# Five spreads of 128 slot rows for seven of 96, and earlier parameter loads, in a two-block transformer kernel

## The chip, the cores and the metric

The kernel runs on one core of a Trainium2 chip, in one launch. The metric is the device time of that launch in microseconds; a smaller number is better. The program is written at the level of the engines' own instruction streams: TensorE (PE) for matmuls, VectorE (DVE), ScalarE (ACT), GpSimd (POOL), and SyncE (SP), whose queue issues the loads of weights. Semaphores tie the streams together.

## The reference

Two blocks of two layers each, in float32, on 256 tokens of width 1024. The first block's layer 0 is a matrix-memory mixer (mLSTM, 4 heads of width 512) with a gated feed-forward, its layer 1 a state-space mixer (S5) with a mixture of 8 experts. The second block has latent attention and a recurrent mixer, each with a gated feed-forward. What the change touches, cut to the core:

```python
def s5_mixer(u, lam_re, lam_im, b_re, b_im, c_re, c_im, d_skip, log_dt, w_glu, b_glu):
    dt = jnp.exp(f32(log_dt))[:, None]
    mag = jnp.exp(lr * dt)
    ar, ai = mag * jnp.cos(li * dt), mag * jnp.sin(li * dt)
    ...
    bbar_re = kr[..., None] * br - ki[..., None] * bi
    ...

def moe_ffn(u, w_router, w13, w2):          # 8 experts, top 2, F = 2816
    logits = (t @ w_router).astype(jnp.float32)
    top_val, top_idx = lax.top_k(logits, TOP_K)
    top_w = jax.nn.softmax(top_val, axis=-1)
    for e in range(N_EXPERTS):
        gate_e = jnp.sum(jnp.where(top_idx == e, top_w, 0.0), axis=-1)
        out = out + gate_e[:, None] * swiglu(t, w13[e], w2[e])
```

## The kernel before, in words

The whole is one long program, stage after stage; activations stay in on-chip memory and 565 MB of weights and inputs stream in once. SyncE loads weight tiles of up to 1 MB into a ring of 6 buffers. The load of a tile waits until TensorE has begun the tile five places before it (`tile_begun`, in `load`). TensorE's order is written out by hand, as is every other engine's.

**The end of the mLSTM and the first feed-forward.** `stage_mlstm` on ScalarE ends with `head_squares` and `head_root` for the last head (L2178 to L2190) and `layer_norm(0)`, whose squares are L2095. VectorE scales each head's output (L2780) and multiplies it (L2783, which signals `h_scaled`). TensorE meanwhile runs the output projection (L1286). `stage_ffn0` on ScalarE (L2203) waits for the first normalized input, issues nine loads (router, B, C and log_dt of the S5 layer, L2206 to L2215), and takes the silus of steps 0 and 1 (L2115). Then `s5_exponentials` (L2192) waits for all nine loads and exchanges values with a chain of small VectorE operations (L2836 to L2869). Only after it come the silus of the later steps. VectorE, too, runs that chain ahead of the product of step 2 (L2638). A step of the feed-forward is 64 matmul records of gate and up (L980) and 32 of the down projection (L1134); the down projection of step s stands behind the gate and up of step s + 1.

**The experts.** `stage_moe` gives each expert 96 slots (`SLOTS`) for the tokens that chose it. `xe` holds the gathered tokens, `wgather` the weight of each token in each slot. TensorE turns `wgather` into `scatterT`, slots on the partitions (L1467), and ScalarE copies it (L2285). If no expert has more than 96 tokens, `few_tokens` runs: the 176 hidden chunks of 128 (22 for each expert) go in 44 quads. A quad has four gate and up tiles (`gate_up`, L1481), three turns of the hidden values (`turn_hidden`, L1492) and two down tiles (`down`, L1505). In each, TensorE's four strips of 32 columns hold 32 slots each, so an expert's output stands as 3 rounds of slots by 4 quarters of the width. ScalarE copies it out (`y_quarters`, L2294) and issues 12 small copies (L2310) that bring it into `ye`, with 96 slot rows on the partitions. One quad later `spread` (L1518) multiplies each of the 8 column chunks of `ye` by the expert's `scatterT`, and VectorE adds the result to `res` (L3054). At expert 0 ScalarE also issues 12 copies of the last expert's scatter matrix (L2305), so that the last expert can be spread straight from `y_quarters` (L1542), with 32 slot rows in each of the array's four strips of rows. In every quad ScalarE's order is: three silus (L2316), the outputs of an expert that has ended, the copy of the turned hidden values (L2320), for which the next down product waits.

A number such as L1481 is the line in the code below. One matmul of the program stands as two records in the trace.

## Time and profile before

| | |
|---|---|
| median of 3 runs | 2809.24 us (2805.33 to 2809.74) |
| the profiled execution, its own time | 2807.94 us |
| its span, first to last instruction | 2806.2 us |
| TensorE busy (matmuls) | 2694.8 us, 96% of the span |
| VectorE, ScalarE, GpSimd busy | 786.1, 404.3, 763.0 us |
| transferred | 565.39 MB, 201 GB/s over the span |
| granted TensorE clock, mean | 0.976 |

The profile is of one execution. All times in its rows are counted from the first instruction. The span is 1.7 us less than the execution's own time, which is what the runs' times are. Busy time of TensorE runs to modelled ends of matmuls, so two groups that follow each other can overlap by a few tenths; where a length matters, starts are subtracted. The granted clock is a share of 2.4 GHz.

### The profile page before, as it was taken

How to read it: one execution, taken by the hardware profiler on the slowest of the kernel's cores; microseconds unless marked ns; L12 is line 12 of the kernel's file. 1: busy time of each engine (PE TensorE's matmuls, PEld its weight loads, DVE VectorE, ACT ScalarE, POOL GpSimd, SP SyncE). 2: the span in 40 equal slices, each digit the busy share in tenths (PEclk: the TensorE clock that was granted, in tenths of full speed). 3: DMA queues.
4: the chain of work that ended last, by engine and by line, in shares of the span. 5: the costliest groups of instructions: out<-in, count | busy, mean ns of one | idle time of the engine just before them, and what ended most of it. 6: DMA issues, size and time to landing. Idle time of an engine off the chain costs nothing.

```text
span 2806.2 us, 52573 instructions
## 1 busy us (share of the span) xinstructions
PE 2694.8 (96%) x23411; PEld 1983.1 (71%) x23411; DVE 786.1 (28%) x1504; ACT 404.3 (14%) x828; POOL 763.0 (27%) x591
## 2 busy tenths in 40 slices
PE   7999999999999999999999898999999989999998
PEld 5756778866655566656655345468888868998998
DVE  3306310064300000000002286132220146432561
ACT  0032010120210000000002244110000031221100
POOL 0051018064000000000000161045555432521886
PEclk9999999989999999999999999999999999998999
DMA  9976444468599999999998320132222242222542
GB/s 305 309 266 229 135 144 150 150 211 306 176 335 368 367 374 384 378 382 382 381 378 301 87 83 1 60 120 91 85 81 83 87 131 94 72 76 76 166 159 98
DMA packets 375012, 565.39 MB, mean 201 GB/s; under 512 B 50136, under 2 KB 205440, under 8 KB 374656
## 3 DMA queue, kind: packets, MB, share of 16 engines
q1 hardware_dynamic: 351504, 554.58, 56.9%
q10 hardware_dynamic: 23280, 7.42, 1.2%
q8 instruction: 186, 3.05, 0.5%
q14 instruction: 42, 0.34, 0.0%
HBM read 557.75 MB, written 1.05 MB: 199 GB/s over the span
## 4 chain that ended last, share of the span: by engine, by line
PE 53%; issue 35%; DMA 3%; POOL 3%; DVE 2%; POOLq 2%; ACT 1%; ACTq 1%; DVEq 1%; SPq 0%
PE psum L980 10%; PE psum L1799 9%; PE psum L2017 5%; PE psum L1836 5%; PE psum L1880 3%; PE psum L1134 2%; PE psum L2045 2%; PE psum L1286 2%; PE psum L1900 2%; PE psum L1621 2%; DMA sv<-in_s_log_dt 2%; PE psum L1021 1%; DMA ring<-in_ada_w 1%; PE psum L1927 1%; POOLq L3600 1%
## 5 line engine op out<-in xcount | busy, mean ns | idle before, releaser
L1481 PE MATMUL psum<-ring,xe 128*32 128x256 f32 x8448 | 465.7, 379 | 1.9 <-issue 1.9
L1481 PEld LDWEIGHTS psum<-ring,xe 128*32 128x32 f32 x8448 | 271.2, 110 | 183.0 <-issue 10.3
L980 PE MATMUL psum<-act_in,ring 128*128 128x256 f32 x1216 | 268.6, 382 | 2.5 <-DVE act_in L2616 1.4
L980 PEld LDWEIGHTS psum<-act_in,ring 128*128 128x128 f32 x1216 | 231.2, 191 | 41.7 <-issue 9.1
L3599 POOL TENSOR_TENSOR cq<-cq,nstat 128x512 f32<-128x512 f32 x3 | 3.7, 1269 | 932.5 <-DVE nstat L3150 932.5
L1505 PE MATMUL psum<-ring,zs 128*32 128x256 f32 x4224 | 239.2, 382 | 4.6 <-ACT zs L2320 4.6
L3061 DVE TENSOR_TENSOR zs<-zs,psum 128x128 f32<-128x128 f32 x132 | 37.9, 288 | 632.3 <-ACT zs L2316 632.3
L1505 PEld LDWEIGHTS psum<-ring,zs 128*32 128x32 f32 x4224 | 138.8, 111 | 96.3 <-issue 7.6
L3612 POOL TENSOR_TENSOR w_sums<-ring 128x512 f32<-128x512 f32 (+1 forms) x34 | 42.2, 1242 | 307.2 <-DVE ctxT L3201 131.3
L1621 PE MATMUL psum<-a,ring 128*128 128x512 f32 x224 | 97.5, 594 | 2.0 <-ACT a L2362 1.3
L2316 ACT ACTIVATE zs<-psum 128x128 f32<-128x128 f32 x132 | 36.4, 278 | 389.4 <-PE psum L1481 389.4
L3150 DVE RECIPROCAL nstat<-nstat 128x512 f32<-128x512 f32 x23 | 76.8, 3345 | 48.7 <-ACT nstat L2086 48.2
L1799 PE MATMUL psum<-a,ring 128*128 128x256 f32 x352 | 82.2, 386 | 4.1 <-DVE a L3121 4.1
L1134 PE MATMUL psum<-zs,ring 128*128 128x256 f32 x352 | 80.3, 387 | 6.0 <-DVE zs L2638 6.0
L1799 PE MATMUL psum<-a,w_sums 128*128 128x256 f32 x352 | 85.0, 385 | 0.7 <-ACT a L2362 0.7
L980 PE MATMUL psum<-a,ring 128*128 128x256 f32 x384 | 83.9, 379 | 0.0
L1621 PEld LDWEIGHTS psum<-a,ring 128*128 128x128 f32 x224 | 42.1, 190 | 56.0 <-issue 51.8
L1799 PE MATMUL psum<-x_rows,w_sums 128*128 128x256 f32 x352 | 79.8, 380 | 0.0
L1134 PEld LDWEIGHTS psum<-zs,ring 128*128 128x128 f32 x352 | 68.4, 195 | 16.0 <-issue 6.4
L980 PEld LDWEIGHTS psum<-a,ring 128*128 128x128 f32 x384 | 72.6, 190 | 9.7
L1799 PEld LDWEIGHTS psum<-a,ring 128*128 128x128 f32 x352 | 67.6, 193 | 14.7 <-DVE a L3121 4.7
L1799 PEld LDWEIGHTS psum<-a,w_sums 128*128 128x128 f32 x352 | 67.9, 193 | 10.9 <-issue 1.4
(549 smaller groups left out, 4228.0 us busy)
## 6 DMA issues: line engine op xcount, KB each, us to landing
ring<-in_moe_w SPq DMA_DIRECT2D x320, 512.0 KB, 7.1
ring<-in_ffn_w SPq DMA_DIRECT2D x97, 1024.0 KB, 5.3
ring<-in_ada_w SPq DMA_DIRECT2D x96, 1024.0 KB, 8.1
ring<-in_moe_w SPq DMA_DIRECT2D x88, 1024.0 KB, 8.3
ring<-in_hg_w_in SPq DMA_DIRECT2D x20, 1024.0 KB, 5.2
ring<-in_mlstm_w_in SPq DMA_DIRECT2D x16, 1024.0 KB, 6.4
ring<-in_moe_w SPq DMA_DIRECT2D x64, 256.0 KB, 5.7
ring<-in_mlstm_w_out SPq DMA_DIRECT2D x8, 1024.0 KB, 5.7
```

Of the source, the lines that this page charges most:

```text
L980: last = pe.matmul(bank(j)[:, n * T:(n + 1) * T], tile[:, k * width + n * P:k * width + (n + 1) * P], src(k), start=start and k == 0, stop ...
L1134: last = pe.matmul(psum[:, NB + n // 2, (n % 2) * T:(n % 2 + 1) * T], ring[:, t % RING, k * D + n * P:k * D + (n + 1) * P], hid[:, i % 2, ...
L1286: last = pe.matmul(bank(j)[:, n * T:(n + 1) * T], ring[:, t % RING, k * 256 + n * P:k * 256 + (n + 1) * P], hT[:, 8 * half + k], start=hal ...
L1481: last = pe.matmul(psum[32 * g:32 * g + 32, r, 0:2 * P].rearrange("p (u n) -> p u n", u=2), xe[:, 2 * i + k, at:at + 32], tile[:, k, :, g ...
L1505: last = pe.matmul(psum[32 * b:32 * b + 32, DOWN + r // 2, (r % 2) * T:(r % 2 + 1) * T], q_hidT[:, q % 2, r, 32 * g:32 * g + 32], ring[:, ...
L1621: last = pe.matmul(bank(j), ring[:, t % RING, at:at + P], src(k), start=k == 0, stop=k == kc - 1)
L1799: last = pe.matmul(product_bank(side, m), held[:, k], moving(k), start=k == 0, stop=k == 3)
L1836: last = pe.matmul(product_bank(q, m), held[:, k, q], moving(2 * kk + k), start=kk == 0 and k == 0 and m in (1, 5, 3, 6), stop=kk == 5, sk ...
L1880: last = pe.matmul(product_bank(side, m), held[:, k], moving(k), start=k == 0, stop=k == 3)
L1900: last = pe.matmul(bank(j)[:, a * T:(a + 1) * T], a2[:, k, tok:tok + P], ring[:, t % RING, k * 256:(k + 1) * 256], start=k == 0, stop=k == ...
L2017: last = pe.matmul(small_bank(side, m), held[:, k], moving(k), start=k == 0, stop=k == 3)
L3150: dve.reciprocal(st, st).then_inc(S("nrstd_ready"), 1)
```

## The change

It does two things.

First, the nine loads for the S5 layer become a function `s5_loads` of their own, called on ScalarE ahead of `layer_norm(0)`, behind a wait for `h_scaled` of all four heads. `ctok` and `bT` exchange their addresses.

Second, the slot rows of all experts are counted through: 8 x 96 = 768 rows are 24 pieces of 32 and 6 chunks of 128. `scatterT` is turned as 6 chunks. The row pieces of experts 0 to 6 but the last one (`KEPT_ROWS` = 20) go to `ye`, now two buffers of 128 rows, and each of the 5 full chunks is spread once its last row has come: behind experts 1, 2, 3, 5 and 6 (`SPREAD_AFTER`). The piece of expert 6 that is left over stays with the three of expert 7 in `y_kept`, and the last spread takes these four pieces. The copies for that (`last_rows`) go out four at a time behind each of the first four quads.

On ScalarE, the end of the mLSTM and the start of the feed-forward. Before (`qk` holds the heads' outputs, `xm` the residual, `zs` the hidden values, `sv`, `ctok`, `bmat` the S5 parameters):

```order
L2190 ACTIVATE bd<-psum,one 128x256
L2095 ACTIVATE xm<-xm 128x512 x4
L2090 ACTIVATE stat<-psum 128x256
L2086 ACTIVATE small<-psum,one 128x2
L2206 DMA router_w<-in_moe_router 128x8x8
L2208 DMA bmat<-in_s_b_re 128x32x16
L2208 DMA bmat<-in_s_b_im 128x32x16
L2211 DMA ctok<-in_s_c_re 128x8x64 x2
L2211 DMA ctok<-in_s_c_im 128x8x64 x2
L2215 DMA sv<-in_s_log_dt 64x32x1 x2
L2115 ACT_TABLE_LOAD
L2115 ACTIVATE zs<-psum 128x512 x2
```

and with the change:

```order
L2214 ACTIVATE bd<-psum,one 128x256
L2193 DMA router_w<-in_moe_router 128x8x8
L2195 DMA bmat<-in_s_b_re 128x32x16
L2195 DMA bmat<-in_s_b_im 128x32x16
L2198 DMA ctok<-in_s_c_re 128x8x64 x2
L2198 DMA ctok<-in_s_c_im 128x8x64 x2
L2202 DMA sv<-in_s_log_dt 64x32x1 x2
L2102 ACTIVATE xm<-xm 128x512 x4
L2097 ACTIVATE stat<-psum 128x256
L2093 ACTIVATE small<-psum,one 128x2
L2122 ACT_TABLE_LOAD
L2122 ACTIVATE zs<-psum 128x512 x2
```

The loads have moved ahead of the four squares (`xm<-xm`) of the layer norm, and the two silus follow the norm directly.

On ScalarE in the experts, the first quads. Before, after six quads without a load:

```order
L2316 ACTIVATE zs<-psum 128x128 x3
L2320 ACTIVATE zs<-psum 128x384
L2316 ACTIVATE zs<-psum 128x128 x3
L2294 ACTIVATE zs<-psum 128x768
L2305 DMA last_scatter<-scatterT 32x256 x12
L2310 DMA ye<-zs 32x256 x12
L2320 ACTIVATE zs<-psum 128x384
L2316 ACTIVATE zs<-psum 128x128 x3
```

and with the change, the first two quads:

```order
L2333 ACT_TABLE_LOAD
L2333 ACTIVATE zs<-psum 128x128 x3
L2337 ACTIVATE zs<-psum 128x384
L2327 DMA last_scatter<-scatterT 32x256 x4
L2333 ACTIVATE zs<-psum 128x128 x3
L2337 ACTIVATE zs<-psum 128x384
L2327 DMA last_scatter<-scatterT 32x256 x4
```

and expert 0's end:

```order
L2333 ACTIVATE zs<-psum 128x128 x3
L2313 ACTIVATE zs<-psum 128x768
L2321 DMA ye<-zs 32x256 x12
L2337 ACTIVATE zs<-psum 128x384
L2333 ACTIVATE zs<-psum 128x128 x3
```

The loads of `last_scatter` stand four at a time behind the turned values' copy (128x384) of a quad, and no longer ahead of the rows' copies at expert 0's end.

On TensorE, the quad behind expert 0. Before:

```order
L1505 MATMUL psum<-ring,zs 32x256 x24
L1481 MATMUL psum<-ring,xe 32x256 x72
L1505 MATMUL psum<-ring,zs 32x256 x48
L1492 MATMUL psum<-cst,zs 128x128 x3
L1518 MATMUL psum<-scatterT,ye 128x256 x8
L1481 MATMUL psum<-ring,xe 32x256 x96
L1505 MATMUL psum<-ring,zs 32x256 x48
```

and with the change:

```order
L1510 MATMUL psum<-ring,zs 32x256 x24
L1486 MATMUL psum<-ring,xe 32x256 x72
L1510 MATMUL psum<-ring,zs 32x256 x48
L1497 MATMUL psum<-cst,zs 128x128 x3
L1486 MATMUL psum<-ring,xe 32x256 x96
L1510 MATMUL psum<-ring,zs 32x256 x48
```

The spread (`scatterT,ye`) of expert 0 is gone there; its rows are in the spread behind expert 1.

The diff, cut to its core:

```diff
+KEPT_ROWS = 3 * (NE - 1) - 1
+SPREAD_AFTER = {(4 * kk + 3) // 3: kk for kk in range(KEPT_ROWS // 4)}
...
+        ctok = sb("ctok", [P, 2, DC, 2, SP_], work)
         bT = sb("bT", [P, 2, DC, P], work)
-        ctok = sb("ctok", [P, 2, DC, 2, SP_], work)
         cmT = sb("cmT", [P, 2, DC, P], work)
...
-        scatterT = sb("scatterT", [P, NE, T], work)
+        scatterT = sb("scatterT", [P, NE * SLOTS // P, T], work)
         xe = sb("xe", [P, DC, NE * SLOTS], work)
-        ye = sb("ye", [P, D], work)
-        last_scatter = sb("last_scatter", [P, 3, T], work)
+        ye = sb("ye", [P, 2, D], work)
+        last_scatter = sb("last_scatter", [P, 4, T], work)
         crowded = work.enter_context(nc.sbuf_tensor("crowded", [P, 1], mybir.dt.int32))
         work.close()
...
+        y_kept = zflat[:, 12 * T:16 * T].rearrange("p (r n) -> p r n", r=4)
+        wgather_slots = wgather.rearrange("p a e s -> p a (e s)")
...
-                for g in range(4):
+                for g in range(3):
                     for i in range(2):
                         for a in range(2):
-                            at = i * T + a * P
-                            last = pe.transpose(psum[0:SLOTS, NB + g, at:at + P], wgather[:, a, 2 * g + i], ident)
+                            at, s0 = i * T + a * P, (2 * g + i) * P
+                            last = pe.transpose(psum[:, NB + g, at:at + P], wgather_slots[:, a, s0:s0 + P], ident)
                     last.then_inc(S("scatterT_full"), 1)
 
...
                     def spread(e):
-                        pe.wait_ge(S("moe_y_turned"), 16 * 12 * (e + 1))
+                        kk = SPREAD_AFTER[e]
+                        pe.wait_ge(S("moe_y_turned"), 64 * min(3 * (e + 1), KEPT_ROWS))
                         for g in range(4):
-                            pe.wait_ge(S("spread_out"), 4 * e + g + 1)
+                            pe.wait_ge(S("spread_out"), 4 * kk + g + 1)
                             for n in range(2):
                                 last = pe.matmul(psum[:, SPREAD + g % 2, n * T:(n + 1) * T],
-                                                 ye[0:SLOTS, (2 * g + n) * P:(2 * g + n + 1) * P],
-                                                 scatterT[0:SLOTS, e], start=True, stop=True)
+                                                 ye[:, kk % 2, (2 * g + n) * P:(2 * g + n + 1) * P],
+                                                 scatterT[:, kk], start=True, stop=True)
                             last.then_inc(S("spread_full"), 1)
 
                     for n, (kind, q, i) in enumerate(EXPERT_TILES):
...
+                    pe.wait_ge(S("last_scatter_in"), 16 * 16)
                     pe.wait_ge(S("moe_y_out"), NE)
-                    pe.wait_ge(S("spread_out"), 2 + 4 * (NE - 1))
-                    for r in range(3):
+                    pe.wait_ge(S("spread_out"), 2 + 4 * len(SPREAD_AFTER))
+                    for r in range(4):
                         for n in range(2):
                             for b in range(4):
                                 rows = slice(32 * b, 32 * b + 32)
-                                last = pe.matmul(psum[:, NB + b, n * T:(n + 1) * T], y_quarters[rows, r, n * P:(n + 1) * P],
-                                                 last_scatter[rows, r], start=r == 0 and n == 0, stop=r == 2,
+                                last = pe.matmul(psum[:, NB + b, n * T:(n + 1) * T], y_kept[rows, r, n * P:(n + 1) * P],
+                                                 last_scatter[rows, r], start=r == 0 and n == 0, stop=r == 3,
                                                  skip_group_check=True)
                     last.then_inc(S("last_spread"), 1)
 
...
                 head_root(NH - 1)
+                s5_loads()
                 layer_norm(0)
...
-            def stage_ffn0():
-
-                act.wait_ge(S("ffn0_in_ready"), 1)
+            def s5_loads():
+
+                act.wait_ge(S("h_scaled"), NH)
                 act.dma_start(router_w[:], w["moe_router"][0].rearrange("(c p) e -> p c e", p=P)).then_inc(S("s5_in"), 16)
                 for i, name in enumerate(("s5_b_re", "s5_b_im")):
                     act.dma_start(bmat[:, i], w[name][0].rearrange("(j g) p h -> (g p) j h", g=2)).then_inc(S("s5_in"), 16)
...
                     act.dma_start(sv[g * SP_:(g + 1) * SP_, 0], log_dt[g:g + 1].broadcast_to([SP_, NPAIR]),
                                  allow_slow_non_contiguous=True
                                  ).then_inc(S("s5_in"), 16)
...
-                for g in range(4):
+                for g in range(3):
                     act.wait_ge(S("scatterT_full"), g + 1)
-                    act.activation(scatterT[0:SLOTS, 2 * g:2 * g + 2],
-                                   psum[0:SLOTS, NB + g].rearrange("p (e t) -> p e t", e=2), ACT.Copy
+                    act.activation(scatterT[:, 2 * g:2 * g + 2],
+                                   psum[:, NB + g].rearrange("p (e t) -> p e t", e=2), ACT.Copy
                                    ).then_inc(S("scatterT_out"), 1)
...
 
                         act.wait_ge(S("moe_y_full"), e + 1)
-                        act.activation(y_quarters.rearrange("p r n -> p (r n)"),
-                                       psum[:, DOWN:DOWN + 2].rearrange("p b n -> p (b n)")[:, 0:3 * T], ACT.Copy
-                                       ).then_inc(S("moe_y_out"), 1)
+                        rounds = psum[:, DOWN:DOWN + 2].rearrange("p b n -> p (b n)")[:, 0:3 * T]
                         if e == NE - 1:
+                            act.activation(y_kept[:, 1:4].rearrange("p r n -> p (r n)"), rounds, ACT.Copy
+                                           ).then_inc(S("moe_y_out"), 1)
                             return
                         if e:
-                            act.wait_ge(S("spread_full"), 4 * e)
-                        else:
-                            act.wait_ge(S("scatterT_out"), 4)
-                            for r in range(3):
-                                for b in range(4):
-                                    act.dma_start(last_scatter[32 * b:32 * b + 32, r], scatterT[32 * r:32 * r + 32, NE - 1]
-                                                  ).then_inc(S("last_scatter_in"), 16)
+                            act.wait_ge(S("moe_y_turned"), 64 * 3 * e)
+                        if e == NE - 2:
+                            act.activation(y_kept[:, 0], rounds[:, 2 * T:3 * T], ACT.Copy)
+                        act.activation(y_quarters.rearrange("p r n -> p (r n)"), rounds, ACT.Copy
+                                       ).then_inc(S("moe_y_out"), 1)
+                        rows = [u for u in range(3 * e, 3 * e + 3) if u < KEPT_ROWS]
+                        if rows[-1] // 4 >= 2:
+                            act.wait_ge(S("spread_full"), 4 * (rows[-1] // 4 - 1))
                         act.wait_ge(S("moe_y_out"), e + 1)
-                        for r in range(3):
+                        for u in rows:
                             for b in range(4):
-                                act.dma_start(ye[32 * r:32 * r + 32, b * T:(b + 1) * T], y_quarters[32 * b:32 * b + 32, r]
-                                              ).then_inc(S("moe_y_turned"), 16)
+                                act.dma_start(ye[32 * (u % 4):32 * (u % 4) + 32, u // 4 % 2, b * T:(b + 1) * T],
+                                              y_quarters[32 * b:32 * b + 32, u - 3 * e]).then_inc(S("moe_y_turned"), 16)
+
+                    def last_rows(r):
+
+                        for b in range(4):
+                            act.dma_start(last_scatter[32 * b:32 * b + 32, r], scatterT[32 * r:32 * r + 32, KEPT_ROWS // 4]
+                                          ).then_inc(S("last_scatter_in"), 16)
 
                     for q in range(QUADS):
                         for r in range(3):
...
                         act.wait_ge(S("moe_turned"), q + 1)
                         act.activation(q_hidT[:, q % 2].rearrange("p r s -> p (r s)"), psum[:, TURNED, 0:3 * P], ACT.Copy
                                        ).then_inc(S("moe_hidden_turned"), 1)
+                        if q == 0:
+                            act.wait_ge(S("scatterT_out"), 3)
+                        if q < 4:
+                            last_rows(q)
                     y_out(NE - 1)
...
                         for g in range(4):
-                            dve.wait_ge(S("spread_full"), 4 * e + g + 1)
+                            dve.wait_ge(S("spread_full"), 4 * SPREAD_AFTER[e] + g + 1)
                             dve.tensor_tensor(res[:, 2 * g:2 * g + 2], res[:, 2 * g:2 * g + 2],
                                               psum[:, SPREAD + g % 2].rearrange("p (a t) -> p a t", a=2), ALU.add
                                               ).then_inc(S("spread_out"), 1)
...
                         for e in ended_by(q - 2):
-                            add(e)
+                            if e in SPREAD_AFTER:
+                                add(e)
```

## Rows read from the trace of the kernel before

**Rows 1.** The page's slices: 40 equal parts of the span, busy tenths, and GB/s.
```profile
PE   7999999999999999999999898999999989999998
...
GB/s 305 309 266 229 135 144 150 150 211 306 176 335 368 367 374 384 378 382 382 381 378 301 87 83 1 60 120 91 85 81 83 87 131 94 72 76 76 166 159 98
```
**Rows 2.** The chain that ended last, 325 to 425 us: start us, us, what.
```profile
352.00 47.11 DMA sv<-in_s_log_dt
399.13 0.24 ACT sv L2196
...
411.69 0.70 DVE zs L2638
```
**Rows 3.** The waits, 320 to 440 us: engine, line, awaited: us, times, longest.
```profile
PE psum L1134 <- DVE zs L2638: 6.0, 1, 6.0
```
**Rows 4.** TensorE's timeline in ffn0: start, us, engine, line, xcount [idle before].
```profile
385.65 7.07 PE L1134 MATMUL psum<-zs,ring 128*128 128x256 f32 x32
392.56 13.98 PE L980 MATMUL psum<-act_in,ring 128*128 128x256 f32 x64
412.52 9.57 PE L1134 MATMUL psum<-zs,ring 128*128 128x256 f32 x32 [5.99 <-DVE zs L2638]
```
**Rows 5.** ScalarE's timeline in the experts, a quiet quad and expert 0's end.
```profile
798.01 0.28 ACT L2316 ACTIVATE zs<-psum 128x128 f32<-128x128 f32 x1 [8.31 <-PE psum L1481]
...
883.11 0.81 ACT L2294 ACTIVATE zs<-psum 128x768 f32<-128x768 f32 x1 [2.31 <-PE psum L1505]
883.11 8.05 ACTq L2305 DMA_DIRECT2D last_scatter<-scatterT  x12
891.21 8.63 ACTq L2310 DMA_DIRECT2D ye<-zs  x12
899.88 0.49 ACT L2320 ACTIVATE zs<-psum 128x384 f32<-128x384 f32 x1 [15.96 <-issue]
```
**Rows 6.** TensorE's timeline behind expert 0.
```profile
888.65 7.95 PE L1481 MATMUL psum<-ring,xe 128*32 128x256 f32 x144
900.52 7.85 PE L1505 MATMUL psum<-ring,zs 128*32 128x256 f32 x96 [3.91 <-ACT zs L2320]
...
908.68 3.80 PE L1518 MATMUL psum<-scatterT,ye 96*128 96x256 f32 x16
912.41 10.57 PE L1481 MATMUL psum<-ring,xe 128*32 128x256 f32 x192
922.80 5.36 PE L1505 MATMUL psum<-ring,zs 128*32 128x256 f32 x96
...
928.57 10.57 PE L1481 MATMUL psum<-ring,xe 128*32 128x256 f32 x192
```
**Rows 7.** The timeline of all engines, 262 to 362 us.
```profile
286.70 1.23 DVE L2783 TENSOR_TENSOR qk<-qk,zs 128x1024 f32<-128x1024 f32 x1
...
328.69 2.42 ACT L2095 ACTIVATE xm<-xm 128x512 f32<-128x512 f32 x4 [45.15 <-DVE xm L2599]
...
335.46 0.39 ACTq L2206 DMA_DIRECT2D router_w<-in_moe_router  x1
...
350.34 8.88 ACTq L2215 DMA_DIRECT2D sv<-in_s_log_dt  x2
```
**Rows 8.** TensorE's timeline at both ends of the expert stage.
```profile
773.74 1.91 PE L1467 MATMUL psum<-cst,xm 128*96 128x128 f32 x16
...
1516.58 5.39 PE L1505 MATMUL psum<-ring,zs 128*32 128x256 f32 x96 [0.67 <-ACT zs L2320]
1522.94 2.87 PE L1542 MATMUL psum<-last_scatter,zs 32*128 32x256 f32 x48 [0.97 <-issue]
```
**Rows 9.** DMA issues at 1264 to 1280 us and at 1290 to 1350 us: median us to landing.
```profile
ring<-in_moe_w SPq DMA_DIRECT2D x1, 1024.0 KB, 12.1
...
ring<-in_moe_w SPq DMA_DIRECT2D x8, 1024.0 KB, 8.5
```
**Rows 10.** Windows of TensorE, PEld, DVE, ACT, POOL busy (x), clock, DMA share, GB/s.
```profile
1283.00:1348.00 65.00, 65.00 (x1180) 38.50 (x1172) 3.64 (x13) 5.62 (x16) 0.00 (x0) 1.00 1.03 388
865.00:882.00 17.00, 17.00 (x312) 10.07 (x308) 0.86 (x3) 1.33 (x4) 0.00 (x0) 1.00 1.04 393
```

34 lines of the change are left out of this document (17 added, 17 removed).

## The prediction

> **What bounds the kernel now.** I read the slices first: TensorE is busy nine tenths or more in nearly every slice [rows 1], so what counts is TensorE's own work and the few places where it stands still. Next the chain of waits and the waits of the two stretches that the change touches, then the timelines of TensorE and ScalarE there, and last the DMA views of the expert stage, because the slices also show the transfers at 370 to 385 GB/s there [rows 1].
>
> In the first feed-forward stage the chain leaves TensorE: the last of the nine parameter loads (log_dt) is issued at 352.0 and lands 47.1 us later. ScalarE's exponential then starts at 399.1, and VectorE's parameter chain runs until the product of step 2 can be formed at 411.7 [rows 2]. TensorE needs that product at about 406.5 (64 records of gate and up take 13.98 us from 392.56) and starts the down projection at 412.52: a wait of 6.0 us [rows 3, 4]. It then takes 9.57 us for what takes 7.07 us elsewhere [rows 4].
>
> In the expert stage a whole quad runs without a gap except after expert 0. There ScalarE issues 12 copies of the last expert's scatter matrix from 883.1 (8.05 us) and 12 copies of the outputs' rows (8.63 us) before it copies the turned hidden values at 899.88 [rows 5]. TensorE wanted them at 896.6 (888.65 + 7.95), waits 3.91 us, and the next 96 records take 7.85 us and not 5.36 us [rows 6].
>
> **Part 1, the early parameter loads.** They now wait for head 3's product on VectorE, which ends at 287.9 (286.70 + 1.23) [rows 7]. Their issue took ScalarE from 335.5 to 359.2, 23.7 us, log_dt's last one included [rows 7]; the same length from 288 ends at 312, 17 us before ScalarE's next work, the squares at 328.7 [rows 7]. This is the one engine that now waits for something new: behind the wait stand only these loads and those squares, and it is over before ScalarE's issue can matter to anyone. If nothing else changes, log_dt lands by about 352 (its last issue begins 16.5 us after the first, so at 304.5, plus 47.1). ScalarE then takes the exponential right behind the second silu, at about 363, and VectorE's chain of 12.4 us (399.1 to 411.5) ends near 378. The product of step 2 needs the gate and up results, which TensorE finishes at 385.65 [rows 4]. So the chain lies under matmuls with 7 us to spare, and the loads have 40 us of slack. Gone are 6.0 us of waiting and 2.5 us (9.57 - 7.07) behind it: **-8.5 us**. What is late next there is nothing that TensorE waits for: GpSimd's products with these parameters only start earlier. The swap of the addresses of ctok and bT moves no work: nothing.
>
> The price of these transfers beside the output projection's weight loads: in the trace they ran beside the feed-forward weights, which TensorE uses at the same pace, and TensorE had no wait on a weight load there. I take nothing. The bounds are 0 and 3.6 us, by which the landing of a weight tile grew beside another burst of ScalarE's copies (below); the output projection has five tiles of 6.9 us between request and use, so I stay at the lower end.
>
> **Part 2, ScalarE's burst.** The 12 (now 16) copies of the last rows go out four at a time behind the first four quads' copies. Four of 0.67 us (8.05 / 12) are 2.7 us, where ScalarE idles 8.3 us before the next quad's first silu [rows 5]. After expert 0 only the row copies remain: copy at 883.11 (0.81 us), 8.6 us of issuing, the turned values copied by 893.1, 3.5 us before TensorE asks. Gone are 3.91 + 2.49 = **-6.4 us**.
>
> **Part 3, fewer spreads.** Seven spreads of 96 slot rows become five of 128, behind experts 1, 2, 3, 5 and 6. One takes 912.41 - 908.68 = 3.73 us [rows 6], 16 records for 8 matmuls. I take the same time with 128 rows, because a full 128x128 product of the same 256 columns takes 7.07 / 32 = 0.22 us per record [rows 4], against 3.80 / 16 = 0.24 here. Two fewer: **-7.5 us**. Bounds for the rows: no change, or in proportion to them (5 x 3.73 x 128/96 = 24.9 us against 26.1), which would leave 1.2 us.
>
> **Part 4, the ends.** Four of 16 transposes go: 4 x 1.91 / 16 = **-0.5 us** [rows 8]. The last spread has 64 records for 48 behind the last expert, where nothing covers it: 16 x 2.87 / 48 = **+1.0 us** [rows 8]. ScalarE's extra copy of a 256-column piece at expert 6 (under 0.5 us, by the 384-column copy of 0.49 us [rows 5]) has 2 us of room before the next down product. The new waits in the row copies (all earlier copies landed, an earlier spread done) are met some 80 us before they are asked, since an expert lasts five and a half quads of 16.16 us. VectorE adds 20 pieces and not 28, which nobody waits for.
>
> **Part 5, what the transfers take back.** A tile is requested when the tile five places before it is begun, so there are about 13.3 us (four gate tiles 10.57, one down tile 2.7) [rows 6]. A 1 MB tile lands after 8.5 us in a long stretch without a spread, and after 12.1 us beside the row copies after expert 4 [rows 9]: 1.2 us are left there, and the spread that stood right behind it goes. The long stretch held 388 GB/s with TensorE never waiting, and 393 is the best stretch that I found [rows 10]. So the transfers keep up with TensorE, but win back only about 1% (0.2 us per quad). After expert 0 and expert 4 the room stays at 1 to 2 us for five quads, and the next burst takes 1 to 3.6 (12.1 - 8.5) more. I take 1 us of waiting in all, **+1.0 us**; bounds 0 and 4 (two bursts of 3.6 less half of what is won back). The one short wait in the stage's rows, 0.67 us, has no slower matmuls behind it (5.39 us for 96 records) [rows 8].
>
> The Trainium skill (DMA: Bandwidth & Descriptors, Where 436 GB/s comes from) says that about 358 GB/s per core binds between HBM and SBUF. By it no part of the expert stage could shrink. The rows of 388 and 393 GB/s speak against it.
>
> **Sum.** -8.5 - 6.4 - 7.5 - 0.5 + 1.0 + 1.0 = -20.9 us. Against the profiled execution's 2807.9 us that is **2787 us**. That execution lies 1.3 us under the median shown, 2809.2, and the three runs spread over 4.4 us. About 0.2% (5.6 us) is what a measurement of this kernel can tell from no change.
>
> **Rivals.**
> *The transfers are the bound.* With the breaks gone the ring runs dry, and parts 2 to 4 come back as waiting for weights. For it: a quad reads four chunks of 1.05 MB (gate and up) and 0.52 MB (down), 6.29 MB, in 16.16 us (912.41 to 928.57), which is 389 GB/s, just what was moved [rows 6, 10]; and the 12.1 us. Against it: 388 GB/s over 65 us without a wait. Only part 1 stays: 2807.9 - 8.5 = 2799 us. Chance 0.12, partial forms included. The figure of the Trainium skill above would bring this case about.
>
> *The parameters still come late or cost elsewhere.* ScalarE's issuing is slowed, or the log_dt pieces delay the output projection. For it: the last piece takes 47 us to land. Against it: the chain could begin 41 us later than the forecast landing and still be done for 406.5 (352 + 41 + 12.4 + a product of 0.7). 2787 + 8.5 = 2795.5 us. Chance 0.06.
>
> *A spread is priced by its rows.* Then 6.3 us less are saved: 2793 us. Against it: the two record times above. Chance 0.04.
>
> *Slower: each burst of row copies starves TensorE.* Lacking the breaks, the room is zero when each of the seven bursts begins. Each would then cost the 3.6 us that landing grows by, and as after expert 0 a wait of that size brings 2.5 us of slower matmuls. Seven times 6.1 is 43 us: 2786 + 43 = 2829 us. It decides from four such bursts on (24 us against 21.9). Against it: five spreads stay, and a landing of 8.5 us leaves 4.8 us of room when a burst begins. Chance 0.03.
>
> *It doesn't do what it says.* Both waits move and don't vanish, say ScalarE's four copies in the early quads delay the turned values and the parameter chain meets the second product: within 5 us of 2808. Chance 0.03.
>
> **How the numbers follow.** The forecast has 0.72. The range runs from 2782 (no waiting for weights, and the runs' own spread) to 2796, which takes in the 4 us of part 5, the rows' price and the late parameters; outside lie most of the transfer-bound case, the slower one and the void one, under 0.2. Faster by over 0.2% are the forecast and the first three rivals: 0.94. Within: 0.03. Slower: 0.03.
>
> **What would show it.** In the profile after, the log_dt issues stand near 305 us, ScalarE's exponential near 363, TensorE has no wait on VectorE before the down projection of step 2, and its 32 records take 7.07 us. In the expert stage the wait on ScalarE after expert 0 is gone, five spreads of 3.7 us stand, and the last spread takes 3.8 us. Waits on weight loads stay under 4 us. I am wrong if TensorE waits for weights in the two long stretches, if a spread takes near 5 us, or if the parameters' loads delay the output projection.

## The result and the profile after

| | before | with the change |
|---|---|---|
| median | 2811.12 us (2805.33 to 2816.99, 9 runs) | 2797.17 us (2787.26 to 2800.72, 9 runs) |
| ratio, 95% interval | | 0.9947 (0.9936 to 0.9958) |
| the profiled execution | 2807.94 us | 2798.92 us |

The change saves 14.9 us (2811.12 x 0.0053), from 11.8 to 18.0 by the interval. The forecast was 20.9 us and 2787 us. The direction was right; the time lies 1.2 us above the range of 2782 to 2796. Two later measurements of the same kernel gave ratios of 0.9934 and 0.9939, so the three point at 15 to 19 us, each known to 3 us or so on either side.

First to the stages. The table takes the first TensorE instruction of each from TensorE's timeline, in us from the start of the span. "Experts" runs from the first gate and up matmul to the transposes behind the last spread. p1, p2 and so on are the experiments below.

```
kernel         output     ffn0     experts  end       ffn0 to   experts,  from there
               projection          begin    of them   experts   length    to the end
before         267.2      335.57   777.57   1525.74   442.0     748.2     1276.9
changed        272.6      340.94   772.43   1513.99   431.5     741.6     1279.6
changed, 2nd   272.3      340.62   773.01   1515.20   432.4     742.2     1274.6
changed, 3rd   272.7      341.45   772.48   1515.59   431.0     743.1     1275.6
p1             270.3      339.02   774.29   1521.24   435.3     747.0     1275.9
p2             273.0      341.32   780.62   1523.05   439.3     742.4     1274.2
filler         272.2      341.04   771.90   1516.04   430.9     744.1     1271.4
late rows      271.7      339.99   774.36   1517.20   434.4     742.8     1278.6
thin copies    272.7      340.98   773.85   1509.05   432.9     735.2     1272.2
more copies    271.7      340.03   774.49   1521.29   434.5     746.8     1271.4
turned         270.9      339.25   775.25   1516.22   436.0     741.0     1276.7
turned, 2nd    272.8      341.16   771.59   1512.13   430.4     740.5     1278.4
```

The stretch up to the output projection is the same code in all of them, and so is the last column. The first differs by up to 5.8 us between single executions, the last by 8.2 us. The profiled execution of before, with 267.2 us, is the shortest of all up to there: p2, whose code ahead of the experts is that of before, took 273.0. So the two profiled executions are 9.0 us apart in all, but 10.5 and 6.6 us in the two stages that the change touches. The column from ffn0 to the experts isn't steady either: it spans 430.4 to 436.0 us among the kernels with the early loads, because what follows the feed-forward in it (the S5 mixer and the router), which the change leaves as it is, varies by a few microseconds. The feed-forward by itself is steady. From its first matmul (ffn0 begin) to the norm behind it (the first `xm,cst` matmul after 560 us) it takes 234.9 to 235.5 us in all ten profiles with the early loads, against 243.55 us in before (579.12 - 335.57) and 241.38 us in p2 (582.70 - 341.32).

**The first feed-forward.** TensorE's timeline of the changed kernel (start, us, engine, line, count, idle before):

```profile
391.08 7.07 PE L1139 MATMUL psum<-zs,ring 128*128 128x256 f32 x32
397.99 13.98 PE L985 MATMUL psum<-act_in,ring 128*128 128x256 f32 x64
411.80 7.07 PE L1139 MATMUL psum<-zs,ring 128*128 128x256 f32 x32
```

The wait of 5.99 us of [rows 4] is gone, and the down projection takes 7.07 us instead of 9.57. ScalarE's timeline shows why:

```profile
307.79 11.27 ACTq L2202 DMA_DIRECT2D sv<-in_s_log_dt x2
334.06 2.42 ACT L2102 ACTIVATE xm<-xm 128x512 f32<-128x512 f32 x4 [45.14 <-DVE xm L2620]
...
363.65 0.60 ACT L2122 ACTIVATE zs<-psum 128x512 f32<-128x512 f32 x1 [13.22 <-PE psum L985]
364.27 1.28 ACT L2220 ACT_TABLE_LOAD   x1
365.56 0.23 ACT L2220 ACTIVATE sv<-sv 128x32 f32<-128x32 f32 x1
```

log_dt is issued from 307.8 us, 42 us before its place in [rows 7], and its last piece lands by 356 (the second of the two is issued at 309.6; the slower takes 46.6 us). The exponential starts behind the second silu at 365.56, and VectorE's last small operation ends at 383.0, 8 us ahead of the product at 391.38. The chain of small operations takes 17.4 us here, not the 12.4 of the trace before (the prediction's 363 and 12.4 don't add up to its 378 either); the room was wide enough for it:

```profile
382.82 0.19 DVE L2857 TENSOR_TENSOR sv<-sv 128x32 f32<-128x32 f32 x1
391.38 0.69 DVE L2659 TENSOR_TENSOR zs<-zs,psum 128x512 f32<-128x512 f32 x1 [8.37 <-PE psum L985]
```

From the output projection to the feed-forward it is 68.3 us in both kernels (340.94 - 272.6, 335.57 - 267.2), and the projection's matmuls themselves take 57.1 us in both: the early loads cost the weights there nothing. In three of the other profiles with early loads the 68.3 are 68.8 us, again with 57.1 us for the projection.

**The experts.** ScalarE's timeline at expert 0's end, to be read against [rows 5]:

```profile
877.97 0.81 ACT L2313 ACTIVATE zs<-psum 128x768 f32<-128x768 f32 x1 [2.31 <-PE psum L1510]
878.81 8.64 ACTq L2321 DMA_DIRECT2D ye<-zs  x12
887.50 0.49 ACT L2337 ACTIVATE zs<-psum 128x384 f32<-128x384 f32 x1 [8.72 <-issue]
```

The turned values are ready at 888.0, and TensorE asks for them at about 892. Its timeline, against [rows 6]:

```profile
883.52 5.36 PE L1486 MATMUL psum<-ring,xe 128*32 128x256 f32 x96
889.21 2.80 PE L1486 MATMUL psum<-ring,xe 128*32 128x256 f32 x48 [0.33 <-DMA ring<-in_moe_w]
892.61 5.39 PE L1510 MATMUL psum<-ring,zs 128*32 128x256 f32 x96 [0.60 <-DMA ring<-in_moe_w]
...
911.97 2.80 PE L1510 MATMUL psum<-ring,zs 128*32 128x256 f32 x48 [0.34 <-DMA ring<-in_moe_w]
...
973.04 2.80 PE L1486 MATMUL psum<-ring,xe 128*32 128x256 f32 x48 [0.92 <-DMA ring<-in_moe_w]
976.57 5.54 PE L1510 MATMUL psum<-ring,zs 128*32 128x256 f32 x96 [0.72 <-DMA ring<-in_moe_w]
982.04 0.55 PE L1497 MATMUL psum<-cst,zs 128*128 128x128 f32 x3
982.42 3.80 PE L1524 MATMUL psum<-scatterT,ye 128*128 128x256 f32 x16
986.15 10.57 PE L1486 MATMUL psum<-ring,xe 128*32 128x256 f32 x192
...
1341.07 2.80 PE L1486 MATMUL psum<-ring,xe 128*32 128x256 f32 x48 [0.39 <-DMA ring<-in_moe_w]
1344.37 2.80 PE L1510 MATMUL psum<-ring,zs 128*32 128x256 f32 x48 [0.50 <-DMA ring<-in_moe_w]
1347.35 2.80 PE L1510 MATMUL psum<-ring,zs 128*32 128x256 f32 x48 [0.18 <-DMA ring<-in_moe_w]
```

The wait on ScalarE has become waits on weights. TensorE stands a few tenths of a microsecond at a time, eight times in all: behind the row copies of expert 0 (issued from 878.8 us), behind those of expert 1 (from 964.3), and behind those of expert 5 (from 1333.3; the waits are at 1341 to 1347 us). Behind expert 4's (from 1249.9) there is none. The list of waits of the whole stage (755 to 1516 us) sums them up, in total, times, longest:

```profile
PE psum L1510 <- DMA ring<-in_moe_w: 2.4, 5, 0.7
PE psum L1486 <- DMA ring<-in_moe_w: 1.6, 3, 0.9
```

In the trace of before TensorE's matmuls have no such row. These 4.0 us are the waits in which the engine visibly stood; in two further profiles of the changed kernel they are 4.3 and 5.6 us. The whole price, with the pauses too short for this list and about 0.2 us that a listed wait costs beyond its length (892.61 - 889.21 = 3.40 us, of which 0.60 are the wait and 2.60 the 48 records), is 6.4 us: 741.6 against the 735.2 us that the stage takes when no weight is late (thin copies, below). Set side by side quad by quad (by the turns of the hidden values), the two kernels differ in three places: 2.1 us behind expert 0's copies, 2.6 us behind expert 1's, 1.7 us behind expert 5's. A spread of 128 rows takes 3.73 us (986.15 - 982.42), exactly what one of 96 took, and the ends are as forecast:

```profile
769.72 1.47 PE L1472 MATMUL psum<-cst,xm 128*128 128x128 f32 x12
...
1510.33 3.73 PE L1549 MATMUL psum<-last_scatter,zs 32*128 32x256 f32 x64 [0.97 <-issue]
```

The transfers, against [rows 9, 10]: DMA issues at 1262 to 1350 us with the median time to landing, then windows of the long stretch behind expert 0 and of that behind expert 4 (busy times and counts of the engines, clock, DMA share, GB/s).

```profile
ring<-in_moe_w SPq DMA_DIRECT2D x43, 512.0 KB, 11.2
ring<-in_moe_w SPq DMA_DIRECT2D x11, 1024.0 KB, 12.1
```
```profile
878.00:980.00 102.00, 98.94 (x1761) 56.75 (x1764) 5.18 (x18) 9.55 (x26) 0.00 (x0) 1.00 1.05 384
1262.00:1350.00 88.00, 86.93 (x1563) 50.26 (x1551) 4.89 (x17) 7.60 (x22) 0.00 (x0) 1.00 1.04 388
```

The 1 MB tiles that took 8.6 us to land in that stretch before now take 12.1. The DMA engines are busy all the time, at 384 to 388 GB/s, where TensorE at full pace asks for 389 (the forecast's own figure).

How late the weights run is best seen from the room that a tile has: from its landing to the first matmul on it. Here it is, in us, for the third gate and up tile of some quads:

```
quad             2     4     6     7     8     10    12    13   |  29    30    32    34    35
before           6.20  4.69  3.50  2.76  9.47  4.73  4.19  5.89 |  2.73  4.50  4.78  4.47  5.60
changed          4.54  3.48  1.19  0.97  0.04  0.51  0.04  4.17 |  3.74  0.84  0.98  0.45  3.57
thin copies      4.00  3.77  2.40  1.57  1.84  1.76  0.82  4.59 |  4.01  3.91  3.15  2.99  6.78
```

Before, the standstill and the spread behind expert 0 gave the transfers 6.7 us of room at once (2.76 to 9.47). With the change, expert 0's 12 row copies (quad 7) meet a room of 1 us, and nothing refills it until the first spread, six quads later, so that expert 1's copies find no room either. In the second stretch expert 4's copies (quad 29) find 3.7 us and use them up without a wait. The room then stays at 0.5 to 1 us, and the next copies, expert 5's, bring the waits.

### The profile page after: what moved, and what is told of

The parts are those of the page before. It is cut to its first block, busy times and chain, and to the rows that moved or that the text cites. A ratio compares the mean times of both kernels' runs of the same rounds, so it can differ in the third digit from the quotient of the medians.

```text
span 2797.1 us, 52526 instructions
## 1 busy us (share of the span) xinstructions
PE 2693.1 (96%) x23391; PEld 1979.4 (71%) x23391; DVE 781.1 (28%) x1496; ACT 404.5 (14%) x828; POOL 762.7 (27%) x591
## 4 chain that ended last, share of the span: by engine, by line
PE 56%; issue 35%; POOL 3%; POOLq 2%; DVE 2%; DMA 1%; ACT 1%; DVEq 0%; SPq 0%; ACTq 0%
PE psum L985 13%; PE psum L1806 9%; PE psum L2024 5%; PE psum L1843 5%; PE psum L1887 3%; PE psum L1139 3%; PE psum L2052 2%; PE psum L1291 2%; PE psum L1907 2%; PE psum L1628 2%; DMA ring<-in_ada_w 1%; PE psum L1026 1%; PE psum L1934 1%; POOLq L3622 1%; PE psum L1744 1%
## 5 line engine op out<-in xcount | busy, mean ns | idle before, releaser
L985 PEld LDWEIGHTS psum<-act_in,ring 128*128 128x128 f32 x1216 | 233.1, 193 | 42.9 <-issue 10.2
L1806 PEld LDWEIGHTS psum<-x_rows,w_sums 128*128 128x128 f32 x352 | 67.2, 191 | 9.3
```

What stands on the lines that cost most here:

```text
L985: last = pe.matmul(bank(j)[:, n * T:(n + 1) * T], tile[:, k * width + n * P:k * width + (n + 1) * P], src(k), start=start and k == 0, stop ...
L1806: last = pe.matmul(product_bank(side, m), held[:, k], moving(k), start=k == 0, stop=k == 3)
```

## The experiments

The theory after the result: parts 1 to 4 of the change do what the sum says, and part 5, the transfers, takes back 6 us and not 1, in two stretches where row copies meet weights that have little room or none. The rivals: the early loads or the split burst yield less than thought; the spreads are dearer; the waits on weights are a cost of the removed breaks alone, whatever is copied.

**Each half by itself.** p1 is the kernel before with part 1 of the change alone (the loads in `s5_loads`, called ahead of `layer_norm(0)`, and the exchanged addresses); p2 is the kernel before with its burst split:

```diff
-                            for r in range(3):
-                                for b in range(4):
-                                    act.dma_start(last_scatter[32 * b:32 * b + 32, r], scatterT[32 * r:32 * r + 32, NE - 1]
...
+                        if q < 3:
+                            for b in range(4):
+                                act.dma_start(last_scatter[32 * b:32 * b + 32, q], scatterT[32 * q:32 * q + 32, NE - 1]
```

> The kernel before, with part 1 alone: the nine loads behind head 3's product, the rest as before. My theory: the parameter chain lies wholly under matmuls, so TensorE's wait before the down projection of step 2 (6.0 us) and the slower 32 records behind it (2.5 us) are gone and nothing else changes: 8.5 us less than before, 0.3%. Rival (the missing microseconds of the whole change were lost here, by transfers beside the output projection or at the start of the program): 3 us less or nothing, and waits on weight tiles between 290 and 340 us.

> The kernel before, with part 2 alone: the 12 copies of the last scatter matrix four at a time behind the first three quads, seven spreads of 96 rows as before. My theory: TensorE's wait on ScalarE after expert 0 (3.9 us) and the slower matmuls behind it (2.5 us) are gone; the spread of expert 0 still stands and gives the weight ring 3.7 us back, so waits on weight tiles come to 1 us at most: 5.5 to 6.4 us less than before. Rival (the first stretch is starved by the copies of rows however the spreads stand): waits on weight tiles of 3 to 4 us there, 2 to 3 us less than before.

p1: ratio 0.9969 (0.9957 to 0.9981), 2803.73 against 2811.88 us. By the ratio this is 8.7 us less (8.5 expected), with an interval from 5.3 to 12.1. p2: 0.9982 (0.9972 to 0.9992), 2806.38 us, by the ratio 5.1 us less (5.5 to 6.4 expected), from 2.2 to 7.9. p2's stage of experts is 5.8 us shorter than before's, and TensorE's timeline says where the last 0.6 us of the 6.4 are:

```profile
891.70 8.00 PE L1481 MATMUL psum<-ring,xe 128*32 128x256 f32 x144
900.27 5.39 PE L1505 MATMUL psum<-ring,zs 128*32 128x256 f32 x96 [0.57 <-DMA ring<-in_moe_w]
```

Taking the standstill away already brings the first wait on a weight. Each of the two profiles also shows the other half's stall a second time, p1 that of the experts and p2 that of the feed-forward:

```profile
897.20 6.66 PE L1505 MATMUL psum<-ring,zs 128*32 128x256 f32 x96 [3.88 <-ACT zs L2323]
```
```profile
416.85 8.82 PE L1134 MATMUL psum<-zs,ring 128*128 128x256 f32 x32 [3.73 <-DVE zs L2638]
```

Here they cost less than in the profile from which the forecast took them: 5.2 us and not 6.4 (3.88 + 6.66 - 5.36), and 6.4 us and not 8.5 (241.38 against 235.0 us for the feed-forward). Both mechanisms are as forecast; what they are worth in a mean execution lies between such pairs, and the intervals can't tell it closer. By the two ratios about 13.8 us are there before a single spread is dropped, of the 15 to 19 that the whole change brings. Dropping them brings only a part of its 7.5 us.

**Matmuls put back where the spreads stood.** If TensorE there waits for weights, eight matmuls that nobody reads should cost almost nothing.

```diff
+                    def filler(e):
+                        pe.wait_ge(S("spread_out"), 2 + 4 * sum(x < e for x in SPREAD_AFTER))
+                        for g in range(4):
+                            for n in range(2):
+                                pe.matmul(psum[:, SPREAD + g % 2, n * T:(n + 1) * T], ident, scatterT[:, 0],
...
+                                    else:
+                                        filler(e)
```

> The changed kernel, with eight matmuls whose result nobody reads in the place of each of the two spreads that were taken out (behind experts 0 and 4), 7.5 us of TensorE's work in all. If the weight ring sets the pace in the two long stretches, these matmuls stand in time in which TensorE would wait for weights anyway: the waits on weight tiles (about 6 us against an unhindered pace) shrink to 1 us or less, and the time grows by 1 to 3 us over the changed kernel. Rival (the ring was not the cause): the time grows by the full 7.5 us.

Ratio 0.9946 (0.9930 to 0.9961), 2797.52 us, beside the changed kernel's 0.9934 to 0.9947 in its three comparisons: no difference that the times can show. In the profile the stage is 1.0 to 2.5 us longer with 7.5 us more of matmuls in it (744.1 against 741.6, 742.2 and 743.1). The list of waits of the stage has a single wait of its matmuls on a weight left, ahead of the filler. With 1.64 us it is more than the 1 us that I expected:

```profile
889.99 2.80 PE L1486 MATMUL psum<-ring,xe 128*32 128x256 f32 x48 [1.64 <-DMA ring<-in_moe_w]
892.78 5.39 PE L1510 MATMUL psum<-ring,zs 128*32 128x256 f32 x96
898.10 0.55 PE L1497 MATMUL psum<-cst,zs 128*128 128x128 f32 x3
898.48 3.62 PE L1533 MATMUL psum<-scatterT,cst 128*128 128x256 f32 x16
902.03 10.57 PE L1486 MATMUL psum<-ring,xe 128*32 128x256 f32 x192
```

So the two spreads that were dropped behind experts 0 and 4 kept TensorE busy in time in which it now mostly waits. This runs against the rival that the spreads are dearer: they are as cheap as forecast, and dropping them there pays 1 to 2.5 us in the stage and not 7.5.

**The last rows' copies somewhere else.** The 16 copies of `last_scatter` stand behind quads 0 to 3, ahead of the first starved stretch. Here they are put behind quads 14, 19, 24 and 25.

```diff
-                        if q < 4:
-                            last_rows(q)
+                        if q in (14, 19, 24, 25):
+                            last_rows((14, 19, 24, 25).index(q))
```

> The changed kernel, with the 16 copies for the last spread not behind the first four quads but behind quads 14, 19, 24 and 25, where a spread has just given the ring some room. If the room that these copies took from the ring in quads 0 to 5 was missing at expert 0's end, about 2 us of the 4 us of waiting in the first long stretch go: 1.5 to 2.5 us less than the changed kernel. Rival (the first stretch is short of transfer capacity whatever it starts with): no change within 0.5 us.

Ratio 0.9944 (0.9927 to 0.9960), 2797.94 us, a stage of 742.8 us. The 2 us that I expected did not come. The waits right behind expert 0 are gone: quad by quad 0.3 us is lost there, where the changed kernel loses 2.1. But others came later: ahead of the first spread, behind expert 1's copies (975 and 979 us), behind expert 2's (1078), behind expert 4's (1263 and 1278) and behind expert 5's (1344 and 1348). The last two groups of moved copies are issued at 1188 and 1204 us, and expert 4's copies at 1250 us then find less room (1.2 us at quad 29, where the table has 3.7): 1.9 us are lost behind them, where the changed kernel loses none. The list of waits sums up to 4.7 us, within the 4.0 to 5.6 of the changed kernel:

```profile
PE psum L1510 <- DMA ring<-in_moe_w: 2.9, 5, 0.7
PE psum L1486 <- DMA ring<-in_moe_w: 1.8, 2, 1.1
```

So moving these copies moves the price and doesn't lower it.

**Copies of almost nothing, and more copies.** These separate the row copies from the missing breaks. In the first all 80 copies to `ye` and all 16 of the last rows are still issued, but each moves 16 columns of 256 (both tiles are cleared first). In the second 12 more copies of full width go out behind quads 7 to 9 and 29 to 31, to the buffer of `ye` that is not in use.

```diff
-                                act.dma_start(ye[32 * (u % 4):32 * (u % 4) + 32, u // 4 % 2, b * T:(b + 1) * T],
-                                              y_quarters[32 * b:32 * b + 32, u - 3 * e]).then_inc(S("moe_y_turned"), 16)
+                                act.dma_start(ye[32 * (u % 4):32 * (u % 4) + 32, u // 4 % 2, b * T:b * T + 16],
+                                              y_quarters[32 * b:32 * b + 32, u - 3 * e, 0:16]).then_inc(S("moe_y_turned"), 16)
```
```diff
+                        for e, q0 in ((0, 7), (4, 29)):
...
+                            if q0 <= q < q0 + 3:
+                                for b in range(4):
+                                    act.dma_start(ye[32 * (q - q0):32 * (q - q0) + 32, (e // 4 + 1) % 2, b * T:(b + 1) * T],
```

> The changed kernel with as many copies between buffers as before, issued at the same places, but each 16 columns wide and not 256 (80 of the experts' output rows, 16 of the scatter matrix), so that the experts' outputs but for these columns are left out of the sum. If the copies' share of the transfer capacity is what empties the weight ring, the 6.4 us of waiting in the expert stage go almost wholly: a stage of 735 to 737 us, 5 to 6 us less than the changed kernel. Rival (the weights alone ask for more than the transfers give in a stretch without a spread): 4 us of waiting or more stay, and at most 2 us are won.

> The changed kernel with 12 more copies of 32 KB in each of the two long stretches, four behind each of the first three quads after experts 0 and 4, into rows that nobody reads. A burst of 12 took the weight queue from 394 to 339 GB/s for 16 us, which is 2.2 us of the ring's time. If the ring is at its capacity there, all of it is waiting: 4.4 us more in the stage (746 us), 3.5 to 5 us more in all. Rival (copies cost only as a burst, by delaying single tiles): spaced like this they cost 1 us or less.

The changed kernel was run again beside them:

> The changed kernel once more, as the measure for the three beside it. In its first profile TensorE began ffn0 5.4 us later than before, and the part behind the experts took 2.8 us longer, where neither kernel differs. If these are chance, both move by some microseconds in this profile; if they come with the change, they stay at 5 and 3 us. The expert stage, from its first gate matmul to the first turn of the context tokens, was 741.6 us and should stay within 2 us of that.

| | median | ratio to before | experts |
|---|---|---|---|
| changed, 2nd | 2795.94 us | 0.9934 (0.9918 to 0.9949) | 742.2 us |
| thin copies | 2788.78 us | 0.9906 (0.9893 to 0.9919) | 735.2 us |
| more copies | 2798.56 us | 0.9944 (0.9931 to 0.9957) | 746.8 us |

Thin copies win 7.2 us by the medians and 7.0 us in the stage, and TensorE has no wait on a weight left in it. 735.2 us is what parts 2 to 4 give without part 5: 748.2 - 6.4 - 7.5 + 1.0 = 735.3 (the transposes stand ahead of the stage). The same sum from p1's profile, whose stall is the shorter one, gives as much: 747.0 - 5.2 - 7.5 + 1.0 = 735.3. More copies make the stage 4.6 us longer, 2.3 us for each 12 (4.4 expected). By the medians it is only 2.6 us (3.5 to 5 expected), with intervals that overlap. The waits on weights grow from the changed kernel's 4.0 to 5.6 us to 7.3:

```profile
PE psum L1486 <- DMA ring<-in_moe_w: 4.2, 7, 1.0
PE psum L1510 <- DMA ring<-in_moe_w: 3.1, 5, 1.3
```

Over 865 to 950 us the transfers of the changed kernel and those of the thin copies, by 40 equal slices of 2.1 us:

```profile
GB/s 387 397 404 389 396 400 386 387 373 348 334 346 376 386 388 387 389 391 406 398 396 391 387 390 387 397 408 398 388 387 389 388 396 404 395 396 393 385 389 393
```
```profile
GB/s 382 403 397 392 403 393 390 382 392 391 394 389 386 385 388 387 399 391 413 393 388 385 387 393 394 402 409 383 387 388 387 398 400 400 397 390 388 384 391 398
```

The dip to 334 GB/s in the first is the burst of 12 copies, whose own 0.39 MB is counted in it; the second has as many copies and no dip. It is the bytes that cost, not the number of copies. In the 16 us around the burst ScalarE's queue holds the DMA engines for 8.6% of the time, 1.4 us:

```profile
q10 hardware_dynamic: 576, 0.39, 8.6%
...
ring<-in_moe_w SPq DMA_DIRECT2D x8, 512.0 KB, 12.1
ring<-in_moe_w SPq DMA_DIRECT2D x2, 1024.0 KB, 13.5
ye<-zs ACTq DMA_DIRECT2D x12, 32.0 KB, 6.1
```

In the same window of the thin copies ScalarE's queue has nearly as many packets (528), but 0.02 MB in them; it holds the engines for 2.2% of the time, and the weight tiles land after 8.8 us (512 KB) and 10.8 us (1 MB). Together with the filler this settles the last rival: with the breaks taken out but no bytes in the copies nothing waits, and with the copies but 7.5 us of matmuls put back a single wait of 1.64 us is left. It takes both, the copies' bytes and the missing breaks.

The Trainium skill (DMA: Bandwidth & Descriptors, Queues, rings and completion order) has each DMA engine go round the queues that have work, a packet at a time. By it a short burst of ScalarE's must push itself between the weights at once, and the landing of 6.1 us for a copy beside 13.5 us for a weight tile agrees with it; no row here shows the order of single packets.

**A version without the copies.** The last rows need no copy if TensorE turns them: 64 records of 32 columns behind expert 0, where it waits anyway, and two copies by ScalarE.

```diff
+                    def turn_last():
+                        for i in range(2):
+                            for r in (2 * i, 2 * i + 1):
...
+                                        last = pe.matmul(psum[32 * b:32 * b + 32, SPREAD + i, at:at + P],
+                                                          wgather_slots[:, a, s0:s0 + 32], ident,
...
+                                    elif e == 0:
+                                        turn_last()
```

> The changed kernel without the 16 copies for the last spread: TensorE makes the four-fold matrix itself, by 32 small matmuls behind expert 0, where a spread stood before, and ScalarE copies it out. This takes 2.9 us of ring time away (16/12 of 2.2 us) and adds about 2 us of matmuls at a place where TensorE waits for weights. If the ring sets the pace, 2 to 3 us less in the stage (739 us) than the changed kernel; rival (matmuls cost what they take): the same time or 1 us more.

Ratio 0.9920 (0.9907 to 0.9934), 2793.33 us: 2.6 us under the changed kernel, 2 to 3 us expected. The intervals overlap, so both were measured again:

> The changed kernel once more, beside the kernel that turns the last rows on TensorE, so that the two are compared on one chip. Both theories expect what two measurements gave: a ratio of 0.993 to 0.995 against the kernel before, 14 to 19 us less. It tells how much of a difference of 2.6 us is the measurement's own.

> The changed kernel with the last rows turned by TensorE behind expert 0 in place of 16 copies, a second measurement. If the copies that are left out were worth it (a stage of experts 1.2 us shorter in the profile, 2.6 us in the medians), the median is again 1 to 4 us below that of the changed kernel on the same chip. If the first difference was chance, the two agree within 1 us or stand the other way round.

The second time 2794.91 us and 0.9939 (0.9925 to 0.9953) for the changed kernel stand against 2795.38 us and 0.9940 (0.9928 to 0.9952) for this one. The stage of experts is 741.0 and 740.5 us long against 741.6, 742.2 and 743.1. The waits on weights sum up to 2.4 and 2.0 us, against 4.0, 4.3 and 5.6. A gain of 1 to 2 us in that stage is likely; in the time of the whole it isn't shown (1 to 4 us were expected again), and no version here that computes the whole beats the changed kernel beyond doubt. Behind expert 0 quads 8 to 11 run without a gap, but the last tile before the spread is still late:

```profile
973.19 2.79 PE L1510 MATMUL psum<-ring,zs 128*32 128x256 f32 x48
976.55 2.80 PE L1510 MATMUL psum<-ring,zs 128*32 128x256 f32 x48 [0.58 <-DMA ring<-in_moe_w]
```

## Why the forecast missed

**Part 1, -8.5 us: right in its mechanism.** Each step stands in the profile: the issue at 307.8 (304.5 forecast), the exponential at 365.6 (363), no wait, 7.07 us. The transfers cost the output projection nothing. That p1 measured -8.7 is closer than it could know, with an interval from -5.3 to -12.1: the feed-forward lost 8.6 us to this wait in one profile and 6.4 in another.

**Part 2, -6.4 us: right in its mechanism.** The stage of p2 is 5.8 us shorter, and its own timeline shows the other 0.6 as a wait on a weight, which belongs to part 5. The size, too, is that of one execution; in p1 the same stall cost 5.2 us.

**Part 3, -7.5 us, and part 4, +0.5 us: right by themselves.** A spread of 128 rows takes 3.73 us, the transposes 1.47 us for 1.91, the last spread 3.73 us for 2.87 (0.9 more, 1.0 forecast). The stage without late weights is 735.2 us long, the sum's 735.3.

**Part 5, +1.0 us: the step that failed.** It is 6.4 us in the profile, 7.0 and 7.9 us in the two repeated ones (742.2 and 743.1 less 735.2), beyond its upper bound of 4. Three things in it were wrong:
- "win back only about 1% (0.2 us per quad)". It rested on a stretch of 17 us at 393 GB/s. What held over 65 us was 388, and a quad needs 389 [rows 6, 10]: nothing is won back. The 388, too, was read where TensorE never waited, so it is what TensorE asked for and shows no reserve. In the table of rooms, before lost 3.4 us from quad 2 to quad 7 without a single copy in the stretch, and thin copies still lose 1.6 us from quad 2 to quad 6. Only breaks refill the room, and the change takes 13.8 us of them away (seven spreads and 6.4 us before, 32.5 us; five spreads after, 18.7 us).
- "the room stays at 1 to 2 us". That was the room of a 1 MB tile beside the old burst. The four copies behind each of the first quads help to bring it to 1 us ahead of expert 0's copies (with these 16 issued later it is about 2 us more), and without the break behind expert 0 it is 0 behind them.
- The bounds counted two bursts, "the next" after expert 0 and after expert 4. Three cost time in the first profile of the changed kernel: expert 0's own 2.1 us, expert 1's 2.6 and expert 5's 1.7. Nor does the 4 follow from its terms: two bursts of 3.6 us are 7.2, and 0.2 us won back in each of some 11 quads is 2.2, half of which leaves 6.1. So the upper bound was mis-sized even by the prediction's own figures, besides the 1 us that was taken within it.

With 6.4 in place of 1.0 the sum is -15.5 us; the three measurements are 14.9, 18.6 and 17.2.

**The level.** 2787 us was set against the profiled execution's 2807.9. The before of the result has a median of 2811.1, and 2811.9 to 2815.6 in the later comparisons. So of the miss of 10.2 us, 5.4 are part 5, 3.2 are the level, and 1.6 lie within the interval (perhaps because parts 1 and 2 were taken from an execution in which both stalls were long; that isn't shown). The first column of the table shows where that execution was short: 267.2 us up to the output projection, where the others took 270 to 273. One profiled execution and three runs did not tell that.

**The rivals.** "The transfers are the bound" named the mechanism, and the truth lies about half-way to it: of the 13.4 us that parts 2 to 4 win (6.4 + 7.5 + 0.5 - 1.0), 6.4 to 7.9 are given back. Its full form did not come about, because 735 us is reached as soon as the copies carry no bytes; that the measured 2797 us stands near its 2799 is luck, since the before of the result lies 3.2 us above the level from which both were counted. The Trainium skill (DMA: Bandwidth & Descriptors, Where 436 GB/s comes from) has about 358 GB/s bind between HBM and SBUF; the rows of 384 and 388 GB/s above exceed that for 102 and 88 us, also without the 8 GB/s or so that are the row copies' own (24 x 32 KB in 102 us). "Each burst starves TensorE" needed four such bursts; three did, at 1.7 to 2.6 us each and not 6.1, and no wait was long enough to slow the matmuls behind it. "A spread is priced by its rows" is excluded by the 3.73 us, the late parameters by p1.

## What to carry to other kernels

Where a stage needs its weights at the very rate at which they come, every pause of the compute engine is the transfers' reserve: before taking pauses out, follow the room from landing to use over the whole stage, and what falls to zero without them comes back as waiting. A rate that is read where the engine never waits is what it asked for; it says nothing of what could be won back. Take it from the longest stretch, not from the best short one. Count the bytes of every other queue too, copies within the on-chip memory included: 12 of 32 KB cost the weights 1.4 to 2.3 us here.

## What was not expected of the hardware

- The same code takes different times in single executions: 267.2 to 273.0 us up to the output projection, and 1271.4 to 1279.6 us from the experts to the end. Between single profiles only stretches that repeat can be compared: here the feed-forward (234.9 to 235.5 us) and the quads of the expert stage (16.16 us each where nothing waits).
- Not every standstill costs more than itself. Behind waits on weights of 0.2 to 1.3 us 96 records of the down projection took 5.39 to 5.72 us in all kernels here (5.36 where nothing waits), and behind waits of 1.6 and 2.0 us 48 took 2.80, at a granted clock of 1.00 in the changed kernel. Behind the 3.9 us on ScalarE the 96 took 7.85 before and 6.66 in p1, at the same stall, and behind p2's 3.73 us on VectorE 32 records took 8.82 and not 7.07. The windows of before:

```profile
896.00:901.00 5.00, 1.09 (x20) 0.43 (x16) 0.43 (x3) 1.00 (x4) 0.00 (x0) 0.77 1.06 346
901.00:909.00 8.00, 8.00 (x101) 4.58 (x94) 0.26 (x2) 0.12 (x1) 0.00 (x0) 0.72 1.03 344
```

and of the changed kernel around its longest waits:

```profile
968.00:976.00 8.00, 6.78 (x120) 3.36 (x112) 0.57 (x2) 1.14 (x4) 0.00 (x0) 1.00 1.05 347
976.00:984.00 8.00, 7.43 (x107) 4.63 (x107) 0.80 (x2) 0.68 (x2) 0.00 (x0) 1.00 1.04 371
```

  A granted clock of 1.00 is 2.4 GHz throughout; a mean of 0.72 is part of the stretch at 1.2 GHz and the rest at 2.4.
- A load of 8 KB from ScalarE's queue (log_dt) takes 42.7 to 48.2 us to land in the eight profiles with the early loads in which the landing was read (46.6 in the first of the changed kernel), and it took 47.1 [rows 2] and 45.7 (p2) when it was issued 42 us later and more. With other weights beside it the time is the same.
